# The expert layer of a three-block kernel: a block's down projection is issued one block later

## What is computed

```
def run(args):
    xb, e = args
    gate, up = jnp.split(xb @ w_gate_up[e], 2, axis=-1)      # [tokens, 1024] @ [1024, 512]
    return (jax.nn.silu(gate) * up) @ w_down[e]              # [tokens, 256] @ [256, 1024]

y = jax.ops.segment_sum(y_buf[dest] * w_s[:, None], tok_s, num_segments=n_tok)
x = x + hier_moe(h, ...)
```

## Time and profile before

| | |
|---|---|
| median of 3 runs | 3050.48 us |
| the profiled execution: time, span | 3050.48 us, 3048.5 us |
| PE busy | 2710.1 us (89% of the span) |
| DVE busy | 1569.6 us (51%) |
| ACT busy | 1045.6 us (34%) |
| mean granted TensorE clock | 0.93 |
| the expert loop, from the first gu matmul to the last add | 705.2 to 977.8 us |

### The profile page before, as it was taken

How to read it: one execution, slowest core, us unless ns; L and a number is a source line. 1 busy time by engine, 2 the same in 40 slices (tenths; PEclk the granted TensorE clock), 3 DMA queues, 4 the chain that set the end, 5 groups by cost and what they waited for, 6 DMA issues and landing times.

```text
span 3048.5 us, 29434 instructions
## 1 busy us (share of the span) xinstructions
PE 2710.1 (89%) x11760; PEld 1948.8 (64%) x11760; DVE 1569.6 (51%) x2840; ACT 1045.6 (34%) x1737; POOL 15.3 (1%) x20
## 2 busy tenths in 40 slices
PE   6988888888998689987994999967989999999997
PEld 2566666663443455555773888845767878878786
DVE  4225563545766656679635444465653323343544
ACT  1034544332112322232423333224663334442222
POOL 0000000000000000000000000000000000000000
PEclk9987888998999889988997999988999999999999
DMA  6111000239995210021131222212212242322220
GB/s 173 42 42 31 20 23 1 83 121 404 389 419 205 92 35 21 21 83 55 56 112 54 83 100 94 83 43 69 83 56 83 83 111 56 97 72 95 83 75 37
DMA packets 178749, 295.99 MB, mean 97 GB/s; under 512 B 26160, under 2 KB 120752, under 8 KB 170416
## 3 DMA queue, kind: packets, MB, share of 16 engines
q1 hardware_dynamic: 175088, 282.52, 26.5%
q0 software_dynamic: 2304, 8.39, 0.7%
q10 hardware_dynamic: 1216, 3.15, 0.3%
HBM read 288.79 MB, written 4.19 MB: 96 GB/s over the span
## 4 chain that ended last, share of the span: by engine, by line
PE 53%; DVE 10%; ACT 3%; issue 1%; DVEq 0%; ACTq 0%
PE ps L316 14%; PE ps L318 14%; PE ps L317 14%; PE ps L324 7%; DVE arena L1843 3%; PE ps L1914 2%; DVE t L369 1%; DVE t L353 1%; PE ps L339 1%; DVE t L2165 0%; PE ps L1936 0%; PE ps L1997 0%; DVE arena L2147 0%; ACT L2574 0%; DVE ws0l L302 0%
## 5 line engine op out<-in xcount | busy, mean ns | idle before, releaser
L302 DVE TENSOR_TENSOR ws0l<-w,ws0h 128x1024 fp32r<-128x1024 f32 (+2 forms) x125 | 135.4, 1083 | 150.5 <-ACT ws0h L294 150.3
L302 DVE TENSOR_TENSOR ws1l<-w,ws1h 128x1024 fp32r<-128x1024 f32 (+1 forms) x124 | 137.8, 1111 | 139.6 <-ACT ws1h L294 139.6
L1843 DVE SCALAR_TENSOR_TENSOR arena<-arena 128x512 f32<-128x512 f32 x240 | 180.3, 751 | 7.4
L324 PE MATMUL ps<-arena 128*128 128x512 f32 (+11 forms) x440 | 151.6, 537 | 28.8 <-DVE arena L1963 24.4
L294 ACT ACTIVATE ws0h<-w 128x1024 fp32r<-128x1024 f32 (+2 forms) x125 | 117.7, 942 | 134.2 <-PE ps L318 130.4
L294 ACT ACTIVATE ws1h<-w 128x1024 fp32r<-128x1024 f32 (+1 forms) x124 | 119.5, 964 | 115.8 <-PE ps L318 108.4
L302 DVE TENSOR_TENSOR ws2l<-w,ws2h 128x1024 fp32r<-128x1024 f32 (+1 forms) x94 | 102.1, 1086 | 89.4 <-ACT ws2h L294 89.4
L324 PE MATMUL ps<-t,con 128*128 128x512 f32 (+1 forms) x68 | 46.2, 775 | 105.0 <-DVE t L353 84.4
L316 PE MATMUL ps<-hpc_hi,ws0h 128*128 128x512 f32 x320 | 128.1, 400 | 6.2 <-DVE ws0l L302 4.1
L316 PE MATMUL ps<-hpc_hi,ws1h 128*128 128x512 f32 x328 | 130.9, 399 | 1.5 <-issue 1.5
L339 PE MATMUL ps<-con,t 128*128 128x128 f32 (+1 forms) x556 | 108.1, 294 | 23.8 <-DVE t L982 7.3
(11 more groups left out here) (531 smaller groups left out, 6197.5 us busy)
## 6 DMA issues: line engine op xcount, KB each, us to landing
w<-in_w_gate_up SPq DMA_DIRECT2D x32, 2048.0 KB, 11.5
w<-in_w_in SPq DMA_DIRECT2D x37, 1024.0 KB, 5.9
w<-in_w_down SPq DMA_DIRECT2D x32, 1024.0 KB, 12.6
w<-in_w_ff SPq DMA_DIRECT2D x16, 2048.0 KB, 8.0
w<-in_w_in SPq DMA_DIRECT2D x13, 2048.0 KB, 8.0
w<-in_w_in SPq DMA_DIRECT2D x48, 512.0 KB, 5.2
w<-in_w_branch SPq DMA_DIRECT2D x6, 2048.0 KB, 7.9
w<-in_w_out SPq DMA_DIRECT2D x4, 2048.0 KB, 8.0
```

The source lines that it names most:

```text
L302: e.go.tensor_tensor(p[1], tiles[t][1], p[0].bitcast(F32), ALU.subtract).then_inc(*e.inc(lo, ("lo", t)))
L324: i = e.go.matmul(bank, lt, rt, start=j == 0, stop=j == n - 1)
L1843: i = e.go.scalar_tensor_tensor(out=cv[:, m, :], in0=ureg[:, m % 2, k:k + 512], scalar=cw[:, m, k:k + 1], in1=cv[:, m, :], op0=ALU.mult, o ...
```

## The change

The down projection of a block is issued one block later, and what follows it moves along. PE issues, after gu(bb), first `turn_x`(bb+1), then `turns` g(bb), then `down(bb-1)`; the `back` pieces woven into gu(bb) are those of bb-2. ACT and DVE follow the same order, with `to_tokens`(bb-1) now ahead of `up(bb)` on DVE. Behind the last block there stand the eight pieces of block 14, `down(15)`, and the eight pieces of block 15. No instruction is added or left out, no buffer changes, and the list of weight loads with its rules stays as it is.

```diff
@@ moe_pe
-                behind = {2: (0, 1, 2), 5: (3, 4, 5), 7: (6, 7)} if bb > b0 else {}
+                behind = {2: (0, 1, 2), 5: (3, 4, 5), 7: (6, 7)} if bb - 2 >= b0 else {}
                 for k in range(8):
                     two_products(...)
                     for d in behind.get(k, ()):
-                        back(bb - 1, d)
+                        back(bb - 2, d)
+                if bb + 1 < b1:
+                    turn_x(bb + 1)
                 e.wait_ge(*dv(("up", bb)))
                 turns(e, [...], ("g", bb))
-                if bb + 1 < b1:
-                    turn_x(bb + 1)
-                down(bb)
+                if bb > b0:
+                    down(bb - 1)
+            for d in range(8):
+                back(b1 - 2, d)
+            down(b1 - 1)
             for d in range(8):
                 back(b1 - 1, d)
@@ moe_act
                 e.go.activation(tm[bb % 2][:, 0:256], ps[2][:, 0:256], ACT.Silu)
+                if bb + 1 < b1:
+                    turned_x(bb + 1)
                 e.wait_ge(*tp(("g", bb)))
                 e.go.activation(tm[bb % 2][:, 256:512], ps[2][:, 0:256], ACT.Copy)
-                if bb + 1 < b1:
-                    turned_x(bb + 1)
-                high(bb)
+                if bb > b0:
+                    high(bb - 1)
...
+            high(b1 - 1)
@@ moe_dve
                 for d in old[3:6]:
-                    add(bb - 1, d)
+                    add(bb - 2, d)
+                if bb > b0:
+                    to_tokens(e, bb - 1)
                 up(bb)
                 for d in old[6:8]:
-                    add(bb - 1, d)
-                to_tokens(e, bb)
+                    add(bb - 2, d)
                 if bb + 1 < b1:
                     weights_of(e, bb + 1)
-                low(bb)
+                if bb > b0:
+                    low(bb - 1)
...
+            for d in range(8):
+                add(b1 - 2, d)
+                if d == 2:
+                    to_tokens(e, b1 - 1)
+            low(b1 - 1)
```

More of the change, by code:

```diff
@@ L1630, in moe_dve @@
             for bb in range(b0, b1):
-                old = range(8) if bb > b0 else ()
+                old = range(8) if bb - 2 >= b0 else ()
                 for d in old[0:3]:
-                    add(bb - 1, d)
+                    add(bb - 2, d)
                 if bb + 2 < b1:
```

## The result

The changed kernel takes 3069.68 us (median of 4 runs, 3068.59 to 3072.71) against 3051.18 us before. The profiled execution took 3073.17 us, with a span of 3071.2 us against 3048.5.

The account below looks back on a forecast made before the run. PE was taken to set the 16.3 us period, with DMA engines also at full load. From 3050.48 us, start -7.8, load round trips +37.4, clock +3 and end +9.3 made +41.9, 3092 us; range 3074 to 3109.

Parts of the forecast that it names:

- The order and the moment of the bursts: On SP's queue: four loads issued within 1.7 us right behind each block's start, nothing else until the next.
- B: Round trip of a block's four weight loads, from issue to PE's start: 19.4 us, ends 18.8 and 20.4.
- The start: First two blocks, without the first down product and back pieces: the third block's gu begins earlier, -7.8 us.
- S(2): Start of gu(2), the gate-up product of block 2: forecast at 729.3 us instead of 737.13.
- The end: From the last block's gu start to the last add: 31.7 us instead of 22.35, +9.3 us.
- PE, ACT and DVE inside a block: Same instructions in another order within each block: cost 0, with up to -7 us kept for `up`'s latency.
- the step from the round trip to the period: Blocks 2 to 15: each of 12 periods becomes the round trip, 19.4 instead of 16.28 us, +37.4 us.
- the clock: Drops of PE's granted clock after waits, in every second block at most, and in angle and last blocks: +3 us.
- the angle block: Block 5, in which DVE computes the angles: longer than the round trip, stays at 23.0 us, 1 us for clock.
- rivals 1 and 3: At gu waits; first: loads no limit, 3052 us, 7%; third: loads' fixed part shows only partly, 3075 us, 15%.

## Why the prediction was wrong, point by point

**Right.** That the change makes the kernel slower, and by the weight loads. The order and the moment of the bursts; B from the end of the down product, 19.4 us forecast, 19.9 for the first burst and 19.5 on the mean. The start: S(2) was forecast 31.96 - 7.8 us behind gu(0)'s start, and came 23.8 behind it (728.37 - 704.60), -8.2. The end: +9.3 forecast, 31.9 - 22.35 = +9.5 measured. PE, ACT and DVE inside a block: 0 was taken, with up to -7 kept; 0.14 us a block, some 2 us, were there once the loads did not hide them. The run with the gate-up loads ahead, in which PE never idles in a block but the one with the angles, shows that `to_tokens` ahead of `up` costs nothing.

**Wrong: the step from the round trip to the period.** The prediction said that a block's transfer "must start and end between S(j+2) and S(j+3)", and that "the period becomes the larger of PE's 16.3 us and this round trip B". The start of the transfer is the end of the down product, which lies ahead of S(j+2) by PE's wait. So the wait is given to the next burst, and two neighbouring blocks pay B - P once between them: 12 x (19.4 - 16.28) = 37.4 us should have been half, 18.7. The measured waits are 18.2. Halved, the sum would have been 3073.7 us, 4.0 above the median and 0.5 above the profiled execution. That it would have come so near is in part luck: of the two terms below, the clock's was 5 us too small and the angle block's 4 us too large.

**Wrong: the clock.** I gave it 3 us, since a slower block would be hidden behind B. But two periods hold PE's own time once, and the clock lost in a block behind a wait is added to it, since it puts off the next C. By the granted clock the drops cost 8.5 us in the 13 blocks (2.9 in the block of 0.85, 5.3 in three of 0.90 and 0.91, and 0.4 in block 2, at whose end the clock fell while PE waited) against 3.4 before, +5. And not every wait had one: behind waits of 3.62, 2.04, 2.40 and 2.43 us the clock was lower, behind 2.39 and 2.46 it was not.

**Wrong: the angle block.** It was to stay at 23.0 us with 1 us more for the clock. It fell to 18.55: DVE began the angles while PE waited 2.39 us for weights, so PE idled 1.12 instead of 3.73 us for the adds, and the clock, which fell there before, stayed at 1.00. -4.4 us, of which 2.5 are busy time that a lower clock had lengthened before. The first instruction of the angles, and PE's wait for the adds:

```profile
785.40 0.48 DVE L385 TENSOR_SCALAR t<-t,con 128x512 f32<-128x512 f32 x1
...
794.25 0.50 PE L324 MATMUL ps<-onehot,yo_hi 128*128 128x512 f32 x1 [1.12 <-DVE x L1624]
```

The 22.0 us between S(2) and S(15) then come apart so. Idle time, +16.3: 18.2 of waits for weights, -2.6 in the angle block's wait for adds, 0.7 in small pieces. Busy time, +5.8: +7.7 in the four blocks whose clock was 0.85 to 0.91, -2.5 in the angle block, and +0.6 in the eight others, which were busy for 16.30 to 16.38 us against 16.27 before. Why these take some 0.2 us more than the 16.14 of the run with the gate-up loads ahead, I have not traced. With the start, -8.2, and the end, +9.5, that is the 23.3 us by which the loop grew; the forecast had 41.9.

**The rivals.** The time fell between rivals 1 and 3, and is neither: the loads were a limit, and B was no smaller than said on the mean. The rule of the Trainium skill ("DMA: Bandwidth & Descriptors", section "Anatomy of one DMA"), a fixed 2.0 us and 436 GB/s, gave 3075 and came nearer to the time, but not by a better path: that sum too had a round trip in every period. The page gives it for transfers that GpSimd issues, and these loads are SP's; by it, as an estimate, the burst takes 17.6 us, where the round trips measured were 18.2 to 21.0, and 18.5 at best on an empty queue. The Trainium skill's passage on a loop that waits for a transfer at each turn ("TensorE: Matmul & The Clock Gate", "HAM oscillation — how this bites in real kernels") was borne out in part: four of the nine blocks that began with a wait had a lower clock.

## What to carry to other kernels

When a product is issued later, look at what its end sets free: in a queue that is strictly in order, the load that waits for it holds back loads whose buffers have long been free, and here that cost some 24 us (ratio 1.0062 against 0.9983 with the free loads ahead), where the reordering itself gave 2 us in the blocks and took 1.3 at the ends. Then write down the times as recurrences, with the issue and the start as two events, before taking the larger of two durations as the period; a wait in one turn is a head start for the next, and a loop like this one, whose burst goes out one turn ahead of its use, pays (B + P) / 2, not B. A fixed piece of work on another engine that stalls such a loop once can be split over several turns: that alone gave a ratio of 0.9984 here and took 6.8 us out of the loop in the profile (265.8 us against 272.6).

## What the runs showed of the hardware

After waits of 2.0 to 2.5 us in an else busy PE, the granted clock fell in three cases and stayed in two in the same profile. The length of the wait alone did not decide it: behind 2.85 us in the run with late loads alone, and behind 2.88 us in the run with more work on PE, the block's clock was 1.00, and behind 2.04 us in the changed kernel it was 0.91. In the run with the half loads, waits of up to 1.84 us left it at 1.00; after waits of 5.0 to 5.6 us in the run with the pause it was low behind each of the first three (means of 0.91 to 0.92 over a pair of blocks). With four loads in one burst and a gather beside it, a round trip of 6.82 MB took from 18.2 to 21.0 us, a spread wider than I had counted on (18.8 to 20.4 from the end of the down product, which lies 0.24 us ahead).
